# Where in SBUF an arena begins: 64 bytes later

## The reference

```python
def hybrid_layer(x, ...):
    proj = (_rms(x) * norm1_g) @ w_in
    ...
    o_a = sliding_window_attention(aq, ak, av, attn_sinks) @ w_attn_o
    o_b = rwkv7_time_mix(rw, ...) @ w_rwkv_o
    o_c = retention(rq, rk, rv, rg) @ w_ret_o
    mixed = g[:, :, 0] * o_a + g[:, :, 1] * o_b + g[:, :, 2] * o_c
    x = x + mixed @ w_out
    h2 = _rms(x) * norm2_g
    x = x + (silu(h2 @ w_ffn_gate) * (h2 @ w_ffn_up)) @ w_ffn_down
```

## Time and profile before

| | |
|---|---|
| median of 3 runs | 3010.15 us (3008.83 to 3012.96) |
| the profiled execution: its span | 3011.2 us (no time beside the span is recorded for it) |
| granted TensorE clock, mean | 0.995 of full speed |
| PE busy | 2969.5 us, 99% |
| matmuls of line 371 | 3 x 2592 on XH/XL, 3 x 976 on HH/HL |
| DMA | 330.94 MB, mean 110 GB/s |

### The profile page before, as it was taken

One profiled execution on the slowest core, in us unless ns is written; L12 is line 12 of the kernel. 1 busy time (PEld: TensorE's weight loads), 2 busy tenths in 40 slices (PEclk: granted clock), 3 DMA queues, 4 the chain that ended last, 5 costly groups with the idle time before them and its releaser, 6 DMA issues.

```text
span 3011.2 us, 52333 instructions
## 1 busy us (share of the span) xinstructions
PE 2969.5 (99%) x20818; PEld 2375.8 (79%) x20818; DVE 1232.2 (41%) x1769; ACT 1094.3 (36%) x1527; POOL 1447.6 (48%) x1824
## 2 busy tenths in 40 slices
PE   9999999999999999999999999999999999999999
PEld 5887778868888777887778888887778777888887
DVE  4826742361110357332647322225833365632210
ACT  4445653243222433124454322224322445432222
POOL 4643345535555355224337555655622333655555
PEclk9999999999999999999999999999999999999999
DMA  6721122213223233225234222233322522422233
GB/s 266 278 86 50 50 98 91 92 49 111 95 96 103 76 110 111 73 76 203 81 112 151 98 98 98 98 104 119 111 70 77 204 81 88 174 98 96 93 104 125
DMA packets 102134, 330.94 MB, mean 110 GB/s; under 512 B 10064, under 2 KB 10448, under 8 KB 101200
## 3 DMA queue, kind: packets, MB, share of 16 engines
q1 hardware_dynamic: 75088, 272.87, 26.7%
q10 hardware_dynamic: 26880, 55.65, 5.0%
HBM read 299.64 MB, written 28.84 MB: 109 GB/s over the span
## 4 chain that ended last, share of the span: by engine, by line
issue 43%; POOL 35%; PE 19%; DMA 1%; POOLq 0%; DVE 0%; ACT 0%; DVEq 0%; SPq 0%; ACTq 0%
POOL w_lo L342 35%; PE psum L371 17%; DMA arena<-in_table 0%; DMA arena<-scratch 0%; POOLq L338 0%; PE psum L486 0%; PE psum L969 0%; PE psum L949 0%; POOLq L348 0%; DMA scratch<-arena 0%; DVE arena L1634 0%; PE psum L963 0%; PE psum L986 0%; DVE arena L2250 0%; PE psum L918 0%
## 5 line engine op out<-in xcount | busy, mean ns | idle before, releaser
L342 POOL TENSOR_TENSOR w_lo<-w_raw,w_hi 128x256 fp32r<-128x256 f32 x1820 | 1447.3, 826 | 1559.2 <-ACT w_hi L1022 1409.7
L371 PE MATMUL psum<-XH,w_hi 128*128 128x512 f32 x2592 | 1050.6, 405 | 12.4 <-DVE XL L1624 6.6
L371 PE MATMUL psum<-XH,w_lo 128*128 128x512 f32 x2592 | 1014.4, 391 | 0.0
L371 PE MATMUL psum<-XL,w_hi 128*128 128x512 f32 x2592 | 1014.4, 391 | 0.0
L1022 ACT ACTIVATE w_hi<-w_raw 128x1024 fp32r<-128x1024 f32 x436 | 460.6, 1057 | 726.0 <-PE psum L371 638.6
L371 PEld LDWEIGHTS psum<-XH,w_hi 128*128 128x128 f32 x2592 | 488.8, 189 | 137.5 <-issue 19.0
L371 PEld LDWEIGHTS psum<-XL,w_hi 128*128 128x128 f32 x2592 | 488.8, 189 | 105.4
L371 PEld LDWEIGHTS psum<-XH,w_lo 128*128 128x128 f32 x2592 | 489.7, 189 | 101.9 <-issue 7.8
L371 PE MATMUL psum<-HH,w_hi 128*128 128x512 f32 x976 | 387.1, 397 | 2.8 <-ACT arena L1416 2.2
L371 PE MATMUL psum<-HL,w_hi 128*128 128x512 f32 x976 | 382.3, 392 | 0.0
L371 PE MATMUL psum<-HH,w_lo 128*128 128x512 f32 x976 | 379.6, 389 | 0.0
(11 more groups left out here) (323 smaller groups left out, 2339.1 us busy)
## 6 DMA issues: line engine op xcount, KB each, us to landing
w_raw<-in_fills SPq DMA_DIRECT2D x456, 512.0 KB, 3.2
scratch<-arena ACTq DMA_DIRECT2D x86, 256.0 KB, 2.1
arena<-in_fills SPq DMA_DIRECT2D x32, 512.0 KB, 4.1
arena<-scratch ACTq DMA_DIRECT2D x10, 1024.0 KB, 7.7
arena<-in_w_ada SPq DMA_DIRECT2D x4, 2048.0 KB, 19.0
H<-scratch ACTq DMA_DIRECT2D x4, 2048.0 KB, 16.7
scratch<-H SPq DMA_DIRECT2D x2, 2048.0 KB, 8.3
arena<-scratch ACTq DMA_DIRECT2D x2, 2048.0 KB, 10.0
```

Source lines behind the costliest of these rows:

```text
L342: ins = nc.gpsimd.tensor_tensor(w_lo[:, to:to + FILL // 4], w_raw[:, of:of + FILL // 4], w_hi[:, to:to + FILL // 4].bitcast(F32), ALU.subt ...
L371: ins = mm(out_ap, wt[:, w:w + 128], xt[:, x0:x0 + T], start=first and k == 0 and o == 0, stop=last and k == n - 1 and o == 2)
```

## The change

The unused tensor `to_line` gets 24 words instead of 8. The arena begins 64 bytes later in every partition, and HH and HL with it. No instruction is added or removed, and no other tensor moves.

```diff
--- before.py
+++ after.py
@@ -175,7 +175,7 @@
         lbs = sb("lbs", 16)
         lbt = sb("lbt", 32)
         small = sb("small", 64)
-        sb("to_line", 8)
+        sb("to_line", 24)
         arena = sb("arena", int(ARENA_KB * KB))
         arena_at = nc.sbuf_base - int(ARENA_KB * KB) * 4
```

## The result

The changed kernel is slower: 3020.79 us, median of 7 runs (3019.83 to 3025.8), against 3011.83 us (3008.83 to 3014.46) for the kernel before, timed beside it. The ratio is 1.0034 with a 95% interval of 1.0024 to 1.0044, 9.0 us more. The forecast was 3003.7 us, 0.22% less, and the range ended at 3012.5. The profiled execution took 3021.15 us, with a span of 3019.4 us.

A forecast was written before the change was run, and what follows sets the result against it. PE was taken as the bound, 99% busy; -6.5 us from HH/HL blocks and 0 from the rest of the arena took the median 3010.15 us to 3003.7 us, range 3002.0 to 3012.5 us.

The forecast's parts named there:

- What bounds the kernel: Whole kernel: PE is busy 99% of the span, so shortening line 371's HH/HL matmul distance shortens the kernel by the same time.
- That HH/HL pay 6.6 ns a block that XH/XL don't, and that this can be had back: Line 371's 976 HH/HL blocks would fall from 686.6 to 680 ns, XH/XL's pace, saving 6.5 us.
- That the offset of 64 in 128 is the cause: HH and HL start 64 bytes past a multiple of 128; moving them onto one removes the extra; chance 0.55.
- The first rival: HH/HL blocks: alignment isn't the cause and nothing changes, 3010.15 us; chance 0.33.
- The second rival: HH/HL blocks: distance to the weights counts, in units of 256 bytes; extra doubles, +6.5 us, 3016.7 us; chance 0.08.
- Weight columns 512 bytes apart and different slots give identical numbers: Argument about HH/HL blocks, held against distance to the weights as the cause, which was priced at +6.5 us.
- 64 bytes are 16 columns: Argument for alignment as the cause: the HH/HL extra of 6.6 ns is 15 columns at XH/XL's pace.
- The rest of the arena costs nothing: Plain fp32 matmuls, VectorE, ScalarE and transfers using the moved arena: 0, with bounds of 1 us either way.

The follow-up runs named there:

- 56 words: Unused tensor to_line given 56 words instead of the 8 of the kernel before, so the arena begins 192 bytes later; 3005.37 us, ratio 0.998.

## Why the prediction was wrong

- *What bounds the kernel*: right. The spans follow the pace of line 371, and no trace of the stages looked at shows a new wait in front of it. One for one it isn't: 11.8 us more for the HH/HL matmuls made the span 8.2 us longer.
- *That HH/HL pay 6.6 ns a block that XH/XL don't, and that this can be had back*: right, and measured by 56 words: 680.1 ns a block, ratio 0.998, where the prediction's sum was 0.9978.
- *That the offset of 64 in 128 is the cause*: this is the step that failed, and the whole sum hung on it. The cause is the distance to the weights in a unit of 256 bytes. The change took the planes from a distance of 64, the cheapest after 0, to 128: from 686.7 to 700.0 ns. 976 x 13.3 ns would be 13 us; 11.8 were measured from start to start, for in the multiplication by `w_out` a block takes 697.3 ns and short stretches don't reach the pattern. Of these, shorter pauses of PE elsewhere gave 3.9 us back in the profiled execution. What in the chip makes the distance count stays open.
- *The first rival*, given 0.33, that the planes' offset plays no part and the time stays at 3010.15 us, fell with the change itself: no instruction differs, and a block takes 13.3 ns more.
- *The second rival*, given 0.08, had the mechanism, the unit and the side: "if the two streams alternate in units of 256 bytes, the planes move from 64 bytes off to 128". Its price of +6.5 us was too small: it let the extra double to 13.2 ns, and it tripled to 20. Its picture that the extra grows with the distance is wrong too: 32 bytes cost 20 ns, 64 cost 6.7.
- *Two arguments were used the wrong way.* "Weight columns 512 bytes apart and different slots give identical numbers" was held against the distance; but 512 bytes, the slots' 4096 and the tiles' 2048 are all multiples of 256, so this could not speak against a unit of 256. And "64 bytes are 16 columns" was taken for a sign of a line of 128 bytes. The extras are 6.7, 13.3 and 20 ns, and 32 bytes cost three times what 64 do, so a count of columns that is like the offset in bytes says nothing of a line of 128.
- *The argument that should have decided.* The prediction wrote down that XH and XL have exactly the offset of w_hi and w_lo, and used it only as a coincidence. XH/XL were the single fast case in the trace, and two things marked them below 2048 bytes: a multiple of 128, and the weights' offset. The trace of before could not tell the two apart, and the forecast gave 0.55 to one of them and 0.08 to the other.
- *The rest of the arena costs nothing*: right. In the changed kernel lines 991 and 993 still take 272/273/273 ns, as in the earlier trace rows, and line 1709 a median of 692, as in the earlier trace rows:

```profile
L991 PE MATMUL psum<-H,arena x128: 272/273/273, 1465.6 to 2550.7; 128*64 128x128 f32 x128
L993 PE MATMUL psum<-arena x128: 272/273/273, 1465.8 to 2550.9; 128*64 128x128 f32 x128
...
L1709 DVE TENSOR_TENSOR arena<-psum,arena x44: 691/692/692, 1679.6 to 2886.9; 128x512 f32<-128x512 f32 x44
```

- The Trainium skill ("SBUF — State Buffer", Who interferes with whom) gives PE an independent read port for the weights and one for the stream; the prediction cited it against the second rival. The traces don't agree that the two addresses are free of each other: with w_lo alone moved by 128 bytes, 693.4 ns a block against 680. They don't show what is shared.

## What to carry to other kernels

Where TensorE streams fp32r planes back to back with a new 128x128 weight block for each matmul, as here, give the streamed planes and all weight planes the same offset below 256 bytes. Alignment of either by itself is not what counts, and a pad that "aligns" can make it worse; the price in this kernel was up to 20 ns in 680, 3%, on every block. The pace is read from the starts, as last less first over the count, and compared between planes; before a cause is named, list everything that the fast case has in common, not only the first thing.

## What was not expected of the hardware

- In all but one of its paces the cost comes in steps of 6.7 ns a block, 16 cycles at the granted 2.4 GHz: 0 at distance 0, one at 64, two with w_lo alone moved by 128, three at 32, 96, 192 and 224, and at 128 in the FFN of the changed kernel.
- It is not symmetrical: 64 over the weights costs 6.7 ns, 64 short (192) costs 20.
- At 128 it is not even fixed: in the FFN 697.0 ns with 16 words between w_lo and H and 700.0 ns in the changed kernel, at the same addresses of HH, HL and the weights, and in the multiplication by `w_out` 700.0 and 697.3. What decides between them stays open, as does why 64 is cheap; neither 160 nor any distance that isn't a multiple of 32 bytes was tried.
